# Attention sums as float32 products in column tiles, with the next chunk's scores in row tiles directly behind them

## The reference

```python
def sink_attention(q, k, v, valid, sinks):
    s = jnp.einsum("bnqhgd,bnkhd->bnhgqk", q, k) * (HEAD_DIM ** -0.5)
    s = jnp.where(valid[None, :, None, None, None, :], s, NEG_INF)
    m = jnp.maximum(jnp.max(s, axis=-1, keepdims=True), sink)
    p = jnp.exp(s - m)
    denom = jnp.sum(p, axis=-1, keepdims=True) + jnp.exp(sink - m)
    p = (p / denom).astype(v.dtype)
    return jnp.einsum("bnhgqk,bnkhd->bnqhgd", p, v)
```

## Time and profile before

| | |
|---|---|
| median of 3 runs | 1311.01 us (1310.81 to 1311.4) |
| the profiled execution, its own time | 1311.2 us |
| its span | 1309.6 us |
| PE busy | 1294.8 us (99%) |
| DVE busy | 750.6 us (57%) |
| ACT busy | 548.1 us (42%) |
| chunks of the first half | from 246 to 500 us |
| chunks of the second half | from 885 to 1124 us |

### The profile page before, as it was taken

How to read it: one execution, slowest core, us unless ns; L and a number is a source line. 1 busy time by engine, 2 the same in 40 slices (tenths; PEclk the granted TensorE clock), 3 DMA queues, 4 the chain that set the end, 5 groups by cost and what they waited for, 6 DMA issues and landing times.

```text
span 1309.6 us, 17847 instructions
## 1 busy us (share of the span) xinstructions
PE 1294.8 (99%) x6341; PEld 1069.5 (82%) x6341; DVE 750.6 (57%) x1189; ACT 548.1 (42%) x1298; POOL 109.2 (8%) x130
## 2 busy tenths in 40 slices
PE   9899999999999999999999999999999999999997
PEld 9788888888888887888888888888888888788886
DVE  6544444576768674346456535357877878433634
ACT  6632222355555553225335222225555555322423
POOL 1121111100000001000001212120000000000000
PEclk9999999999999999999999999999999999999999
DMA  8511111110110115434542211110001000333452
GB/s 342 193 49 49 48 48 48 48 34 33 33 33 33 33 33 177 160 129 159 168 138 82 80 48 48 48 48 33 33 33 49 33 33 34 110 121 109 157 174 99
DMA packets 30417, 109.90 MB, mean 84 GB/s; under 512 B 3424, under 2 KB 3456, under 8 KB 30368
## 3 DMA queue, kind: packets, MB, share of 16 engines
q1 hardware_dynamic: 22032, 79.18, 17.6%
q0 software_dynamic: 8336, 30.05, 6.7%
HBM read 96.63 MB, written 12.58 MB: 83 GB/s over the span
## 4 chain that ended last, share of the span: by engine, by line
PE 97%; DMA 1%; DVE 1%; ACT 1%; issue 0%; POOL 0%; POOLq 0%
PE ps L1039 19%; PE ps L1040 19%; PE ps L1041 18%; PE ps L1280 9%; PE ps L1281 9%; PE ps L1279 9%; PE ps L1193 3%; PE ps L1226 2%; PE ps L1249 1%; PE ps L1250 1%; PE ps L1251 1%; DMA xr<-in_x 1%; PE ps L1050 1%; PE ps L1076 1%; PE ps L1100 1%; PE ps L1101 1%
## 5 line engine op out<-in xcount | busy, mean ns | idle before, releaser
L1039 PE MATMUL ps<-zh,wsplit 128*128 128x512 f32 x1072 | 423.1, 395 | 0.1
L1040 PE MATMUL ps<-zl,wsplit 128*128 128x512 f32 x1072 | 418.5, 390 | 0.0
L1041 PE MATMUL ps<-zh,wsplit 128*128 128x512 f32 x1072 | 417.9, 390 | 0.0
L715 DVE TENSOR_TENSOR wsplit<-wraw,wsplit 128x1024 fp32r<-128x1024 f32 x132 | 196.5, 1489 | 233.5 <-ACT wsplit L455 233.5
L1039 PEld LDWEIGHTS ps<-zh,wsplit 128*128 128x128 f32 x1072 | 201.2, 188 | 46.6 <-DVE wsplit L715 0.6
L1041 PEld LDWEIGHTS ps<-zh,wsplit 128*128 128x128 f32 x1072 | 201.3, 188 | 43.4
L455 ACT ACTIVATE wsplit<-wraw 128x1024 fp32r<-128x1024 f32 x132 | 140.7, 1066 | 226.8 <-PE ps L1281 214.6
L1040 PEld LDWEIGHTS ps<-zl,wsplit 128*128 128x128 f32 x1072 | 201.4, 188 | 40.8
L1280 PE MATMUL ps<-wsplit,gsh 128*128 128x512 f32 x512 | 202.7, 396 | 0.0
L1279 PE MATMUL ps<-wsplit,gsh 128*128 128x512 f32 x512 | 199.3, 389 | 0.3 <-DVE gsl L969 0.3
L1281 PE MATMUL ps<-wsplit,gsl 128*128 128x512 f32 x496 | 196.9, 397 | 0.0
(11 more groups left out here) (153 smaller groups left out, 1344.2 us busy)
## 6 DMA issues: line engine op xcount, KB each, us to landing
wraw<-in_wo SPq DMA_DIRECT2D x64, 512.0 KB, 3.3
wraw<-in_wa SPq DMA_DIRECT2D x36, 512.0 KB, 3.2
wraw<-wc SPq DMA_DIRECT2D x16, 512.0 KB, 3.2
wraw<-in_wb SPq DMA_DIRECT2D x16, 512.0 KB, 3.2
rows<-in_x POOLq DMA_DIRECT2D x16, 512.0 KB, 4.2
xr<-in_x POOLq DMA_DIRECT2D x12, 512.0 KB, 5.6
curaw<-in_wu SPq DMA_DIRECT2D x8, 512.0 KB, 7.9
wc<-cout POOLq DMA_DIRECT2D x8, 512.0 KB, 7.7
```

Source lines behind the costliest of these rows:

```text
L715: ve.tensor_tensor(wl[:, slot, 0:size], wraw[:, slot, 0:size], wh[:, slot, 0:size].bitcast(F32), ALU.subtract).then_inc(w_lo, 1)
L1039: te.matmul(ps[:, PB[bank], :], w_h, rhs_z(zh, tb, k), start=k == 0, stop=False)
L1040: te.matmul(ps[:, PB[bank], :], w_h, rhs_z(zl, tb, k), start=False, stop=False)
L1041: last = te.matmul(ps[:, PB[bank], :], w_l, rhs_z(zh, tb, k), start=False, stop=k == KT - 1)
```

## The change

The sums of the probabilities over the 128 window keys become plain float32 products, one for each key head. Their weights `vw[:, kv, :]` are 128 x 64, and they write 64 partitions of the bank each. The copies of the transposed probabilities stay float32 (`pt`), and so do the values (`vw`), so DVE makes neither `ptl` nor `vl`. The sum over the meta keys (`ptm`) comes first, and still as one float32r product. The next chunk's scores move from ahead of the last 15 matmuls of block 1 to behind the sums.

```diff
@@ ScalarE, attend_group @@
-                        sc.activation(vh[lo_p:hi_p, 0:4:3, :], vtok[lo_p:hi_p, 2 * g + sub // 2, :].rearrange("p (k d) -> p k d", k=2),
-                                      ACT.Copy).then_inc(vw_hi, 1)
+                        sc.activation(vw[lo_p:hi_p, :, :], vtok[lo_p:hi_p, 2 * g + sub // 2, :].rearrange("p (k d) -> p k d", k=2),
+                                      ACT.Copy).then_inc(vw_in, 1)
...
-                            sc.activation(pth[:, kv, :], ps[:, PTB[kv], :], ACT.Copy).then_inc(pt_hi, 1)
+                            sc.activation(pt[:, kv, :], ps[:, PTB[kv], :], ACT.Copy).then_inc(pt_hi, 1)
@@ VectorE, attend_group @@
-                        dve.wait_ge(vw_hi, n + 1)
-                        ve.tensor_tensor(vl[lo_p:hi_p, 0:4:3, :], vtok[lo_p:hi_p, 2 * g + sub // 2, :].rearrange("p (k d) -> p k d", k=2),
-                                         vh[lo_p:hi_p, 0:4:3, :].bitcast(F32), ALU.subtract).then_inc(vw_lo, 1)
...
-                        for kv in range(2):
-                            dve.wait_ge(pt_hi, 4 * n + kv + 1)
-                            ve.tensor_tensor(ptl[:, kv, :], ps[:, PTB[kv], :], pth[:, kv, :].bitcast(F32), ALU.subtract)
                         dve.wait_ge(pt_hi, 4 * n + 4)
@@ TensorE, attend_group @@
                         transposes(0).then_inc(t_done, 1)
+                        project(slot, 1, SOFTMAX_STEPS, KT)
+
+                        pe.wait_ge(pt_lo, n + 1)
+                        pe.wait_ge(vw_in, n + 1)
+                        ob = ps[:, OB, :]
+
+                        te.matmul(ob, vmeta[0:96, :], ptm[0:96, :], start=True, stop=False)
+                        for kv in range(2):
+                            i = te.matmul(ps[kv * HD:kv * HD + HD, OB, :], vw[:, kv, :], pt[:, kv, :], start=False, stop=True)
+                        i.then_inc(o_done, 1)
 
                         if not (last_group and sub == 3):
                             scores(n + 1, 4 * g + sub + 1)
-                        project(slot, 1, SOFTMAX_STEPS, KT)
-
-                        pe.wait_ge(pt_lo, n + 1)
-                        pe.wait_ge(vw_lo, n + 1)
-                        ob = ps[:, OB, :]
-                        for kv in range(2):
-                            v_h = vh[:, 2 * kv:2 * kv + 2, :].rearrange("p a d -> p (a d)")
-                            v_l = vl[:, 2 * kv:2 * kv + 2, :].rearrange("p a d -> p (a d)")
-                            te.matmul(ob, v_h, pth[:, kv, :], start=kv == 0, stop=False)
-                            te.matmul(ob, v_h, ptl[:, kv, :], start=False, stop=False)
-                            te.matmul(ob, v_l, pth[:, kv, :], start=False, stop=False)
-                        te.matmul(ob, vmeta[0:96, :], ptm[0:96, :], start=False, stop=True).then_inc(o_done, 1)
```

More of the change, by code:

```diff
@@ L95, in build @@
         r_at = cursor[0]
-        pth, pth_at = place("pth", [P, 2, TB], F32R)
-        ptl, _ = place("ptl", [P, 2, TB], F32R)
+        pt, pt_at = place("pt", [P, 2, TB])
         ptm, _ = place("ptm", [P, TB], F32R)
@@ L124, in build @@
         warm, _ = place("warm", [P, KPITCH], F32R)
-        vh, _ = place("vh", [P, 4, HD], F32R)
-        vl, _ = place("vl", [P, 4, HD], F32R)
+        vw, _ = place("vw", [P, 2, HD])
         vmeta, _ = place("vmeta", [P, P], F32R)
@@ L183, in build @@
         ks_in = sem("ks_in")
-        vw_hi, vw_lo = sem("vw_hi"), sem("vw_lo")
+        vw_in = sem("vw_in")
         u_in, u_sum, u_pool, u_halo = (sem("u_" + n) for n in ("in", "sum", "pool", "halo"))
@@ L330, in _ @@
             gp.memset(kw[:, :], 0.0).then_inc(s_done, CREDIT)
-            gp.memset(vh[:, :, :].bitcast(F32), 0.0).then_inc(o_gate, CREDIT)
-            gp.memset(vl[:, :, :].bitcast(F32), 0.0).then_inc(o_done, CREDIT)
+            gp.memset(vw[:, 0, :], 0.0).then_inc(o_gate, CREDIT)
+            gp.memset(vw[:, 1, :], 0.0).then_inc(o_done, CREDIT)
             def load_tables(h):
@@ L413, in _ @@
                 gp.tensor_tensor(gsl_first[:, :], gates[:, 0, 0:TB], gsh[:, 0, :].bitcast(F32), ALU.subtract).then_inc(gs_first, 1)
-                pool.wait_ge(vw_lo, NCH * (h + 1))
+                pool.wait_ge(vw_in, NCH * (h + 1))
                 pool.wait_ge(pb_done[1], USES * (h + 1))
@@ L931, in attend_group @@
                         split_lo(block_b(h, g, sub + 1), (sub + 1) % 2)
-                        slot = sub % 2
-                        lo_p, hi_p = slot * CH, slot * CH + CH
-                        dve.wait_ge(vw_hi, n + 1)
-                        ve.tensor_tensor(vl[lo_p:hi_p, 0:4:3, :], vtok[lo_p:hi_p, 2 * g + sub // 2, :].rearrange("p (k d) -> p k d", k=2),
-                                         vh[lo_p:hi_p, 0:4:3, :].bitcast(F32), ALU.subtract).then_inc(vw_lo, 1)
                         if h == 0 and sub < 2:
                             meta_sum(ubuf[:, PRE - META:PRE], 2 + 2 * g + sub)
-                        for kv in range(2):
-                            dve.wait_ge(pt_hi, 4 * n + kv + 1)
-                            ve.tensor_tensor(ptl[:, kv, :], ps[:, PTB[kv], :], pth[:, kv, :].bitcast(F32), ALU.subtract)
                         dve.wait_ge(pt_hi, 4 * n + 4)
```

## The result

The changed kernel takes 1335.68 us (median of 4 runs, 1335.51 to 1337.53), the kernel before 1310.91 in the same comparison. The ratio is 1.0196, with a 95% interval from 1.018 to 1.0213: slower, by 1.8 to 2.1%. The forecast was 1334.3. The profiled execution took 1335.74 us, with a span of 1334.0.

What follows compares the result with a forecast made beforehand. The prediction took TensorE as the bound, busy for 1294.8 of 1309.6 us. Its terms, 10.8 - 1.0 + 13.4 = 23.2 us on the profiled 1311.2, gave 1334.3 us, with a range from 1319 to 1364.

Steps and rivals of the forecast that it cites:

- The chain behind the transposes keeps its length: Transposes, ACT's copies and DVE's `ptm` take as long as before, so every chunk's first sum starts at 4.31 us.
- Column tiles side by side: The two heads' float32 sums run at once on the array, taking 0.87 us per chunk.
- one after another: Rival: the array takes one head's float32 product at a time, +27.8 us, 1362; chance 0.16.
- half side by side: Rival: only the inner two of the four float32 records overlap, +13.9 us, 1348; chance 0.10.
- Changing to column tiles ... I take 0.: At the float32 sums, switching the array to column tiles costs nothing, as read from `project_meta` with 32 columns.
- a gap of 0.2 us at the column tiles: Sign that the prediction is wrong: TensorE shows this gap where it changes to the sums' column tiles.
- The softmax behind the scores: Later scores delay DVE's division, so TensorE waits before the transposes in 12 chunks of `sub` 1 and 2; +13.4 us.
- The wait of the `pmeta` transpose for L814: In `sub` 2, L816 must free bank 6 before this transpose: 0.17 us more each, 1.4 in total.
- DVE keeps up: Rival: the chain from scores to division is shorter than read, so the 13.4 us fall away, 1321; chance 0.12.
- Chunks 15 and 31: Their order doesn't change, and the cheaper sums save 0.52 us each, -1.0 us together.
- The sum: The forecast's total: 10.8 for the order, -1.0 for chunks 15 and 31, 13.4 for softmax stalls, making 23.2 us.
- The rival on the faster side: Copies finish before TensorE's 15 matmuls, so sums start at 3.57 us; 1306.8; chance 0.05 shared with all saved.

Runs made afterwards that it cites:

- The full-width form: From the kernel with the new sums and the scores where they were: zeros widen each float32 sum's weights to the full array; 1319.92 us, ratio 1.008.
- the nearly empty tile: In the kernel with the new sums and the scores where they were, head 1's float32 sum covers 32 of 512 columns; 1302.83 us, ratio 0.9943.
- the scores elsewhere: The changed kernel with the next chunk's scores back ahead of the 15 matmuls; 1304.64 us, ratio 0.9951; measured again, 1303.94 us.

## Why the prediction was right

It held in its total, its mechanism and its places. One term was mis-sized, and others made up for part of it.

- **The chain behind the transposes keeps its length.** Right. The first sum starts at 4.31, the number read from chunk 15. The wait is 0.6 us in 32 chunks. The meta sum last removes it and gives 22 us back.
- **Column tiles side by side.** Right. In the changed kernel the float32 sums take 1.01 us up to the scores, where 0.87 + 0.09 was put, and their records start in pairs. The full-width form costs 0.5 us more per chunk, the nearly empty tile saves nothing. The rivals of one after another and of half side by side are excluded.
- **"Changing to column tiles ... I take 0."** This step failed. `project_meta` with its 32 columns shows no gap, but the 64-column tiles do. With the scores elsewhere the three sums took 1.34 + 0.11, and without any change of mode they would be 0.23 + 0.87: 0.35 per chunk. In the changed kernel it is less: from the float32 sums it is 1.01 us to the row tiles of the scores and 1.01 to the full array elsewhere, so the way out falls together with the way into the row tiles. There the next chunk starts at 6.92 instead of the 6.80 that the sum had without its last 0.11, so +0.48 per chunk and not +0.36: 14.4 us for 10.8. The rule of the Trainium skill, "TensorEngine Tiling (Array Packing)", Key Properties, that a change of mode drains the array, was the better guide here than the one row of 32 columns. Why that row has no gap stays open. By the prediction's own sign, a gap of 0.2 us at the column tiles, this term is wrong with the scores elsewhere (0.35) and not quite in the changed kernel (0.12 in all).
- **The softmax behind the scores.** Right in its places, all 12. The waits for the division measured 8.8 us, and the first transposes come 0.84 to 1.02 us late in `sub` 1 (1.13 put) and 0.74 to 0.90 in `sub` 2 (0.94 put), by the step from the last projection. The maxima begin at 7.04 (6.92 put), and the division's end, put 1.93 later, came 1.89 later. The wait of the `pmeta` transpose for L814 was put at 0.17 in each `sub` 2 and is 0.16 (1.09 for 0.93). The run without the trailing sums gives 12.3 us back, where 13.4 was put; with no wait for the division left there, the rival that DVE keeps up is out.
- **Chunks 15 and 31.** From the first sum to what follows they take 1.44 instead of 1.74 (in chunk 15, 509.19 to 510.63), but the second product behind comes after 0.33 (at 510.96) instead of 0.23. That is -0.2 each and not -0.5, again by the change of mode.
- **The sum.** Between the first and the last chunk's moment 0, the 15 steps of each half grew by 11.7 and 15.2 us, together 26.9 where 10.8 + 13.4 = 24.2 was put: 14.4 for the order, and 12.5 left for the stalls. The stretches before, between and behind the two are 1.2, 1.1 and 0.2 us shorter. Of these 2.5 us the change explains some 0.4, in chunks 15 and 31. The 1.2 before the first chunk lie where the two kernels differ only in the size of a buffer that GpSimd clears: TensorE's waits for `xr` there are 2.8 us in the one trace and 1.5 in the other, and moment 0 of the first chunk lies anywhere from 256.1 to 258.4 us in the ten traces. So part of the closeness of 1334.3 to 1335.7 is luck. The forecast's own terms, 1311.2 + 23.2, give 1334.4 and not 1334.3, which changes nothing.

The rival on the faster side, that the wait for `ptm` goes and the time is 1306.8, can be compared with the run that removed it, though by another way, with the float32 sums in front: 1313.8. Even then the order with the scores behind is not faster, since the 12 waits and the changes of mode stay.

## What to carry to other kernels

Cheaper products on the engine that is the bound gain only if what stands between its waits stays as long: here the scores and 15 projections were the cover of a 4.3 us chain through ACT and DVE. Taking 1.3 us of scores from in front of the sums cost more than the sums saved. Before moving an instruction back, look at who starts with it (here the softmax of the next chunk) and how much time that one had to spare, place by place in the loop; and put the product that waits longest last, behind those whose inputs are there.

A place in the trace that already runs in the new order, such as a loop's last turn, was worth more here than an estimate: it gave the 4.31 to the hundredth.

## What the runs showed of the hardware

- A float32 product of 512 columns at 2.4 GHz (granted clock 0.998 to 0.999) shows two records, and on the full array they start 0.43 us apart. Two such products in two column tiles of 64 take 1.01 us up to the start of what follows, and 1.00 us if the second has 32 columns.
- Going into 64-column tiles cost 0.10 us in front, about 0.05 at the first records and 0.09 behind, with 0.11 more from the first matmul behind to the second. For 32-column tiles with float32r operands the trace showed none of this: 0.22 in front, and 0.23 from the first matmul behind to the second (444.10 to 444.33 in the kernel before).
